# RWKV rounds of a decoder trunk on one core: the state's decay through TensorE, and more copies on ScalarE

## What is computed

```python
def rwkv7_recurrence(r, w, k, v, a, b, s0):
    def step(s, inp):
        r_t, w_t, k_t, v_t, a_t, b_t = inp
        sa = jnp.einsum('bhij,bhj->bhi', s, a_t)
        s = s * w_t[:, :, None, :] + sa[..., None] * b_t[:, :, None, :] + v_t[..., None] * k_t[:, :, None, :]
        return s, jnp.einsum('bhij,bhj->bhi', s, r_t)
...
y = ((y - mean) * lax.rsqrt(var + R_LN_EPS)).reshape(bsz, t, R_WIDTH) * ln_w + ln_b
bonus = jnp.sum(rh * kh * r_k, axis=-1, keepdims=True) * vh
y = y + bonus.reshape(bsz, t, R_WIDTH)
return (y * g) @ w_out, p[:, -1], s_fin
```

## Time and profile before

| | before |
|---|---|
| median of 3 runs | 4311.3 us (4311.24 to 4314.79) |
| the profiled execution's own time | 4307.08 us |
| its span from first to last instruction | 4305.3 us |
| granted clock of TensorE over the span | 0.963 |
| RWKV rounds in the span | about 2235 to 2850 us |
| busy in the span: PE, DVE, ACT | 92%, 57%, 35% |

### The profile page before, as it was taken

How to read it: one execution, slowest core, us unless ns; L and a number is a source line. 1 busy time by engine, 2 the same in 40 slices (tenths; PEclk the granted TensorE clock), 3 DMA queues, 4 the chain that set the end, 5 groups by cost and what they waited for, 6 DMA issues and landing times. The chain is left out here.

```text
span 4305.3 us, 84625 instructions
## 1 busy us (share of the span) xinstructions
PE 3955.7 (92%) x35797; PEld 3633.6 (84%) x35797; DVE 2449.4 (57%) x4964; ACT 1510.7 (35%) x2733; POOL 155.9 (4%) x153
## 2 busy tenths in 40 slices
PE   8799999999989999889968888869988899999998
PEld 4689999999988888889957777749868889999997
DVE  3345656332278886358857878746542464444446
ACT  2113232221177554334325545424521342111112
POOL 0000000000011111000000000000012000000000
PEclk9899999989999999999979999979999999999999
DMA  4323232243455554646631111042323031111102
GB/s 180 106 78 88 91 88 92 81 105 104 119 156 151 152 142 121 175 147 197 204 133 35 33 33 33 19 154 85 117 65 125 22 103 59 49 45 40 50 30 81
DMA packets 374279, 418.69 MB, mean 97 GB/s; under 512 B 49178, under 2 KB 315980, under 8 KB 373036
## 3 DMA queue, kind: packets, MB, share of 16 engines
q1 hardware_dynamic: 361615, 368.01, 28.1%
q0 software_dynamic: 7680, 27.97, 2.2%
q10 hardware_dynamic: 4608, 17.30, 1.0%
HBM read 289.10 MB, written 121.77 MB: 95 GB/s over the span
## 5 line engine op out<-in xcount | busy, mean ns | idle before, releaser
L245 PE MATMUL bank<-xn_hi,pw_whi 128*128 128x352 f32 (+1 forms) x2184 | 732.5, 335 | 20.5 <-PEq L54 8.8
L245 PE MATMUL bank<-xn_hi,pw_wlo 128*128 128x352 f32 (+1 forms) x2184 | 709.3, 325 | 0.0
L245 PE MATMUL bank<-xn_lo,pw_whi 128*128 128x352 f32 (+1 forms) x2184 | 708.8, 325 | 0.0
L245 PEld LDWEIGHTS bank<-xn_hi,pw_whi 128*128 128x128 f32 (+1 forms) x2184 | 414.8, 190 | 38.7 <-issue 24.4
L245 PEld LDWEIGHTS bank<-xn_lo,pw_whi 128*128 128x128 f32 (+1 forms) x2184 | 416.1, 191 | 3.3 <-issue 2.2
L245 PEld LDWEIGHTS bank<-xn_hi,pw_wlo 128*128 128x128 f32 (+1 forms) x2184 | 414.6, 190 | 1.3
L258 ACT ACTIVATE ring<-bank 128x352 f32<-128x352 f32 (+1 forms) x273 | 125.8, 462 | 502.2 <-PE bank L245 501.8
L3148 PE MATMUL bank<-bx_hi,bp_whi 128*128 128x384 f32 (+1 forms) x768 | 273.3, 356 | 30.9 <-DVE bx_lo L3206 18.3
L1797 PE MATMUL bank<-sum_x_hi,pw_whi 128*128 128x352 f32 x768 | 255.7, 333 | 38.7 <-DVE sum_x_lo L1776 23.2
L3769 PE MATMUL bank<-bx_hi,bp_whi 128*128 128x384 f32 (+1 forms) x768 | 251.3, 327 | 4.7 <-issue 4.7
L3769 PE MATMUL bank<-ml_hidden_hi,bp_whi 128*128 128x384 f32 (+1 forms) x768 | 254.5, 331 | 0.0
(11 more groups left out here) (687 smaller groups left out, 10415.9 us busy)
## 6 DMA issues: line engine op xcount, KB each, us to landing
ring<-in_w_in_dram SPq DMA_DIRECT2D x90, 512.0 KB, 4.8
proj_scratch<-ring SPq DMA_DIRECT2D x66, 528.0 KB, 2.9
m_seg<-acum_scratch SPq DMA_DIRECT2D x32, 512.0 KB, 6.8
ring<-in_mlp_w_dram SPq DMA_DIRECT2D x16, 1024.0 KB, 5.5
ring<-in_mlp_w_dram SPq DMA_DIRECT2D x32, 512.0 KB, 3.5
gates_scratch<-ring SPq DMA_DIRECT2D x24, 528.0 KB, 5.0
merged_scratch<-sum_gate ACTq DMA_DIRECT2D x24, 528.0 KB, 5.1
m_raw<-proj_scratch SPq DMA_DIRECT2D x24, 512.0 KB, 5.5
```

Source lines behind the costliest of these rows:

```text
L245: last = self.nc.tensor.matmul(ps[0:n, 0:m], w[:, q, 0:n], self.pair[x][:, q, t0:t0 + m], start=q == 0 and j == 0, stop=q == KD - 1 and j ...
```

## The change

In the scan the decayed state is no longer made by VectorE. TensorE adds eye x ST to the bank in which it accumulates K x V and B x U, and ScalarE takes the sum out, scaled by PC, as the new state. K x V moves from the chunk's first slot to its second. At a new head pair the products with the zero state are left out, with the memset. The copy SO goes to ScalarE, in front of its copy of y.

In the inversion the copies DY (of `square`) and F (of `turn`) go from VectorE to ScalarE, DY ahead of A2 and F ahead of G. In `Prepare` the shifted exponential is read from the unshifted one stored with a leading 1 (`ex`), so that one subtraction on VectorE and one exponential on ScalarE go; V is written by the token shift directly, without ScalarE's copy; the scaling with k_a becomes an activation in slot 6; the zeroing of `raw` comes in slot 6 of the round before. In `Finish` the mean is taken off by the product itself (`centre`), ScalarE squares and copies from PSUM, and two operations of VectorE are left for the affine step and the bonus, where there were three.

```diff
-             ("turn", "va"), ("cross1", "v"), ("cross2", "v"), ("cross3", "v")]
+             ("turn", "a"), ("cross1", "v"), ("cross2", "v"), ("cross3", "v")]
...
+        elif slot == 6:
+            act.wait_ge(self.a_ready, r + 1)
+            act.wait_ge(self.mixed, 3 * r + 3)
+            activation(T[7], T[2], ACT.Copy, scale=k.col["rwkv_k_a"][:, j:j + 1]).then_inc(self.a_scaled, 1)
         elif slot == 7:
             self.nc.scalar.preload_act_table_set("natural_log_exp_and_others")
             act.wait_ge(self.cum, r + 1)
-            activation(T[3], T[1], ACT.Exp, scale=-KAPPA)
+            activation(v.ex[:, :, 1:1 + RC], T[1].rearrange("p (c t) -> p c t", t=RC), ACT.Exp, scale=-KAPPA)
             activation(T[4], T[1], ACT.Exp, scale=KAPPA).then_inc(self.decays, 1)
...
-        elif slot == 9:
-            act.wait_ge(self.shifted, r + 1)
-            activation(T[0], T[0], ACT.Exp, scale=-KAPPA).then_inc(self.exps, 1)
-        elif slot == 18:
...
-            activation(v.V[:, r % 3, :, :], v.pm[:, 2, :].rearrange("p (c t) -> p c t", t=RC), ACT.Copy).then_inc(self.v_made, 1)
...
         if step == "square":
             dve.wait_ge(self.as_[p], evacuated(r, s - 1, "a"))
-            tt(x.DY[:, :, RC:2 * RC], x.D[:, :, :], mask(v.eye), ALU.add)
+            tt(x.DY[:, :, RC:2 * RC], x.D[:, :, :], mask(v.eye), ALU.add).then_inc(self.vs[p], 1)
+            return
...
-        elif step == "square":
-            last = copy(x.DY[:, :, 0:RC], view(b0))
...
-        elif step == "turn":
-            last = copy(x.F[:, :, :], view(b0))
...
         elif step == "square":
+            copy(x.DY[:, :, 0:RC], b0)
             last = copy(x.A2[:, :, :], b1)
...
         else:
+            copy(x.F[:, :, :], b0)
             last = copy(x.G[:, :, :], b1)
...
-                pe.wait_ge(self.s_off, self.updates(r, c))
-                pe.wait_ge(self.kx_mm, n + 1)
-                heads(mm, both[:, 0:RC], AR[:, 0:RC], ST, start=False, stop=True).then_inc(self.r_mm, 1)
-                swapped(mm, state[:, 0:RC], K, V, start=True, stop=False)
-                swapped(mm, o, V, KX[:, RC:2 * RC], start=True, stop=False).then_inc(self.kv_mm, 1)
+                if n % 16 == 0:
+                    swapped(mm, both[:, 0:RC], KX[:, 0:RC], V, start=True, stop=True).then_inc(self.r_mm, 1)
+                else:
...
+                    pe.wait_ge(self.s_off, self.updates(r, c))
+                    pe.wait_ge(self.kx_mm, self.carried(n))
+                    heads(mm, both[:, 0:RC], AR[:, 0:RC], ST, start=False, stop=True).then_inc(self.r_mm, 1)
+                    heads(mm, state[:, 0:RC], v.eye, ST, start=True, stop=False).then_inc(self.st_mm, 1)
+                swapped(mm, o, V, KX[:, RC:2 * RC], start=True, stop=False).then_inc(self.vk_mm, 1)
...
-        if slot == 0 and not w:
-            self.nc.vector.memset(now, 0.0).then_inc(self.s_off, 1)
...
+        elif c < 8 and sub == 2:
+            act.wait_ge(self.s_mm, 8 * r + c + 1)
+            self.nc.scalar.activation(v.ST[:, (c + 1) % 2, :], self.k.bank[1][:, 0:RC], ACT.Copy, scale=v.PC[:, r % 3, c:c + 1]).then_inc(self.s_off, 1)
         elif slot == 24:
+            if r % 2:
+                act.wait_ge(self.turned, r // 2 + 1)
...
+                self.nc.scalar.activation(v.SO[:, :], self.k.bank[1][:, 0:RC], ACT.Copy).then_inc(self.t_off, 1)
             act.wait_ge(self.read, 8 * r + 8)
```

More of the change, by code:

```diff
@@ L1037, in vector @@
         nc.vector.memset(v.reset[:, 0:RW:RC], 0.0)
+        nc.vector.memset(v.ex[:, :, 0:1], 1.0)
         dve.drain().then_inc(self.ones_made, 1)
-        nc.vector.tensor_scalar(v.rest[:, :], k.col["rwkv_mu"][:, 0:24], -1.0, 1.0, ALU.mult, ALU.add)
+        nc.vector.tensor_scalar(v.rest[:, 0:24], k.col["rwkv_mu"][:, 0:24], -1.0, 1.0, ALU.mult, ALU.add)
+        nc.vector.tensor_scalar(v.rest[:, 24:32], k.col["rwkv_k_a"], -1.0, 1.0, ALU.mult, ALU.add)
         for h in HEADS:
@@ L1183, in tensor, with scalar @@
             heads(self.nc.tensor.matmul, bank, v.ones, T[6], start=True, stop=True).then_inc(self.bon_sum, 1)
-    def scalar(self, act, r, slot, read):
+    def scalar(self, act, r, slot):
         if not 0 <= r < ROUNDS:
@@ L1239, in vector @@
             dve.wait_ge(self.scaled, 3 * r + slot - 2)
-            stt(out=pm[:, i, :], in0=raw[:, i, 1:1 + RW], scalar=v.rest[:, i * 8 + j:i * 8 + j + 1], in1=(T[1], D[1], D[2])[i],
+            if i == 2 and r >= 3:
+                dve.wait_ge(read, 8 * (r - 2))
+            stt(out=V if i == 2 else pm[:, i, :], in0=raw[:, i, 1:1 + RW], scalar=v.rest[:, i * 8 + j:i * 8 + j + 1], in1=(T[1], D[1], D[2])[i],
                 op0=ALU.mult, op1=ALU.add).then_inc(self.mixed, 1)
@@ L1244, in vector @@
             dve.drain()
+            if r % 2 and r + 1 < ROUNDS:
+                self.nc.vector.memset(raw[:, :, 0:1], 0.0).then_inc(self.zeroed, 1)
             self.nc.vector.tensor_tensor_scan(out=T[1], data0=v.reset[:, :], data1=T[0], initial=0.0, op0=ALU.mult, op1=ALU.add).then_inc(self.cum, 1)
[L1246 to L1251, removed]
         elif slot == 9:
-            dve.drain()
-            stt(out=T[7], in0=T[7], scalar=1.0, in1=pm[:, 1, :], op0=ALU.add, op1=ALU.mult)
+            dve.wait_ge(self.a_scaled, r + 1)
+            stt(out=T[7], in0=T[7], scalar=v.rest[:, 24 + j:25 + j], in1=pm[:, 1, :], op0=ALU.add, op1=ALU.mult)
         elif slot == 10:
@@ L1448, in tensor @@
                 heads(mm, both[:, 0:RC], N, v.R, start=True, stop=True).then_inc(self.u_mm, 1)
-                pe.wait_ge(self.kv_mm, n + 1)
-                heads(mm, o, ST, AR[:, RC:2 * RC], start=False, stop=False)
+                pe.wait_ge(self.vk_mm, n + 1)
+                if n % 16:
+                    heads(mm, o, ST, AR[:, RC:2 * RC], start=False, stop=False)
+                    pe.wait_ge(self.st_mm, self.carried(n))
+                elif r:
+                    pe.wait_ge(self.t_off, r // 2)
+                swapped(mm, state[:, 0:RC], K, V, start=n % 16 == 0, stop=False).then_inc(self.kv_mm, 1)
             else:
                 pe.wait_ge(self.u_off, n + 1)
+                pe.wait_ge(self.kv_mm, n + 1)
                 heads(mm, state[:, 0:RC], B, v.U, start=False, stop=True).then_inc(self.s_mm, 1)
@@ L1463, in vector @@
             return
[L1464 to L1485 removed]
+        v, c, sub = self.v, slot // 3, slot % 3
+        if c < 8 and sub == 0:
+            dve.wait_ge(self.r_mm, 8 * r + c + 1)
+            self.nc.vector.tensor_copy(v.R[:, :], self.k.bank[0][:, 0:RC]).then_inc(self.r_off, 1)
     def scalar(self, act, r, slot, stored):
@@ L1528, in tensor @@
             pe.wait_ge(y_off, r + 1)
-            heads(self.nc.tensor.matmul, bank, v.ones, v.y[:, r % 2, :], start=True, stop=True).then_inc(self.summed, 1)
+            heads(self.nc.tensor.matmul, bank, v.centre, v.y[:, r % 2, :], start=True, stop=True).then_inc(self.summed, 1)
         elif slot == 19:
@@ L1566, in scalar @@
         if slot == 17:
-            act.wait_ge(self.centred, r + 1)
-            self.nc.scalar.activation(v.F[0], v.y[:, r % 2, :], ACT.Square).then_inc(self.squared, 1)
+            act.wait_ge(self.summed, r + 1)
+            self.nc.scalar.activation(v.F[0], self.k.bank[7][:, :], ACT.Square).then_inc(self.squared, 1)
+            self.nc.scalar.activation(v.y[:, r % 2, :], self.k.bank[7][:, :], ACT.Copy).then_inc(self.centred, 1)
         elif slot == 20:
@@ L1626, in _ @@
                     scan.scalar(act, q - 1, slot, finish.stored)
-                    prepare.scalar(act, q + 1, slot, scan.read)
+                    prepare.scalar(act, q + 1, slot)
                     finish.scalar(act, q - 2, slot)
```

80 lines of the change are left out of this document (28 added, 52 removed).

## The result

| | before | after |
|---|---|---|
| median of 4 runs each | 4311.84 us (4311.24 to 4314.79) | 4258.31 us (4257.57 to 4263.01) |
| profiled execution's own time | 4307.08 us | 4258.98 us |
| its span | 4305.3 us | 4257.3 us |
| granted clock over the span | 0.963 | 0.966 |

The ratio is 0.9877, 95% interval 0.986 to 0.9894. The kernel is 53.5 us faster by the medians and 48.1 us by the profiled executions; forecast were 41.2.

A forecast was written before the change was run, and what follows sets the result against it. TensorE's walk through its slots, with its waits, was taken to bound the rounds. Terms -33.6, -4.5, +0.4 and -3.5 sum to -41.2 us on 4307.1; plus 4.2 to the median, about 4270 us, range 4246 to 4300.

The forecast's parts named there:

- Term 1: At a new head pair, dropping memset and zero-state products gains 4.8 us at each of seven transitions: -33.6 us.
- Term 2: In an ordinary round, four parts sum to -0.3 us, over fifteen rounds with a state: -4.5 us.
- The wait behind the table load: In each round TensorE waits for ScalarE's state of chunk 2, queued behind table load and copies: +1.0 us.
- F in front of G: In a round's last slots ScalarE's U for chunk 5 comes 0.27 later: +0.2 us a round.
- The late slots: Late in a round, TensorE's stops for the state and R go as VectorE's queue shortens: -1.9 us a round.
- Term 3: Ramp and tail of the rounds: +0.4 us for the ramp, -3.5 us for the tail.
- the tail: Last rounds, where the finish is alone: shorter finish, SO copy gone from VectorE, earlier R copy: -3.5 us.
- The ramp: First rounds: k_a scaling and longer inversion copies +1.4, first memset gone -1.0: +0.4 us.
- The transition stays long: Rival: at a pair's start SO, y, table load and U arrive last; two thirds of 5.2 us stay, 4296; chance 0.12.
- The new wait lowers the clock: Rival: TensorE's idling behind the table load lowers the clock each round, 48 us lost, 4318 us; chance 0.08.
- ScalarE's queue takes the state at each chunk: Rival: each chunk's state waits behind wide activations on ScalarE; at 0.6 us a chunk 4347; chance 0.06.
- TensorE alone is left: Rival: late waits and small gaps all go, a round is TensorE's busy time, about 31.5 us: 4246 us; chance 0.12.

The follow-up runs named there:

- e1: Kernel before with only the head pair's start changed (no zero-state products or memset, raw zeroed a round early): 4287.75 us, ratio 0.9936.
- e9: Kernel before with four extra pairs of 384 columns, results unused, where TensorE stands at a new head pair: 4302.56 us, ratio 0.9979.
- e14: Changed kernel with the DY copy alone back on VectorE, run again for a trace: 4253.42 us, ratio 0.9858.
- e11: Changed kernel with the F copy alone back on VectorE: 4258.38 us, ratio 0.9883.
- e7: Kernel before with the changed head pair's start and Finish, and SO on ScalarE; state, DY, F and Prepare as before: 4260.72 us, ratio 0.9881.
- e6: Changed kernel with the state made by VectorE again, without the product with eye: 4265.96 us, ratio 0.9892.
- e8: Changed kernel with the two exponentials one slot later and both copies, DY and F, back on VectorE: 4253.2 us, ratio 0.9855.
- e5: Kernel before with nine extra pairs of 384 columns, results unused, where TensorE stands at a new head pair: 4325.89 us, ratio 1.0027.

## Why the prediction was right, and what was off in it

The time lies in the range and on the forecast's side, 11.7 us below 4270. The sum of -41.2 splits by the trace into four stretches:

| stretch | forecast | measured |
|---|---|---|
| first to fourth scan instruction | about 0 | -1.8 |
| twelve intervals | 6 x 4.8 + 12 x 0.3 = -32.4 | -39.9 |
| sixteenth scan instruction to the next stage's table load | -4.8 - 0.6 - 3.5 = -8.9 | -9.3 |
| the rest of the program | 0 | +2.8 |

The third row is 94.88 us before and 85.61 after. ScalarE's timelines have its end, first of the kernel before, then of the changed one:

```profile
2850.41 1.28 ACT L3960 ACT_TABLE_LOAD   x1 [6.18 <-PEq L54]
```

```profile
2800.43 1.28 ACT L3954 ACT_TABLE_LOAD   x1 [5.68 <-PEq L54]
```

The last row is what is left of -48.1; the stages ahead of and behind the rounds are not changed. The error is in the twelve intervals, and in two terms.

**Term 1, the new head pair.** A transition cost 38.33 - 33.43 = 4.9 us before, and costs nothing now (32.28 against 32.83). The gain is 4.9 + 0.55 = 5.45 us each, above my upper bound of 5.2, where I took 4.8. The 0.4 that I held back for SO and y was not there: SO takes 0.22 us in ScalarE's queue, but TensorE's wait behind it is 0.26, and two products fewer stand on TensorE. 0.65 us, six times, is 3.9 of the 7.5 us that are missing. Two of the reasons behind the 4.8 need correcting. I wrote that nothing then distinguishes a long round from a short one but two products and the SO copy; e1 shows that the finish does, by 1.3 us, until it is shortened. And I had the slow clock as a second payment at every transition, of 3 us by the rival's price; e9 shows 2.0 us at three of six and 0.1 at the others, because the clock is low for some 7 us at the former only, and ScalarE's chain to U hides the first part of it. The term did not suffer from it, since it was taken from the mean of the long intervals and not from a price of the clock.

**Term 2, an ordinary round.** -0.3 forecast, -0.6 measured: the other 3.6 us. By parts:
- The wait behind the table load is there as described: 1.34 us in the row above, 18.6 us in 16 waits. I had DY's share in it as 2 x 0.28 = 0.56; e14 measures 0.57. The load takes 1.28 us and the exponential starts 1.30 us after the load's start (2522.74, 2524.04). The Trainium skill, "ScalarE: Activation LUTs", What ACT_TABLE_LOAD costs, gives 1283 ns for the load and 1380 ns more for a drain: the trace agrees with the first and shows nothing of the second.
- F in front of G was to cost 0.2; e11 shows no cost (1.4 us in twelve rounds the other way, within the disturbances).
- The late slots: their waits are gone, as forecast. But I credited nearly all of it to the state's move and 0.2 to the finish. e7 has the old state and the old copies, and its short rounds are down from 33.4 to 32.6, where e1, without the new finish, has 33.4: the finish is worth 0.8 us a round, and did by itself most of what I laid to the move. For the state's move my terms were +0.6 for the eye products, +0.4 for its share behind the load and -1.9 for the late slots, -0.9 in all; in this kernel it is worth 0.28 at most (e6). The step that failed is the mis-sizing of these two, -0.9 and -0.2 where 0.28 at most and 0.8 were measured, and with it the sentence "VectorE itself is relieved by some 8 us a round, but little of that is on the path". By the windows the relief is 158.2 / 200 x 35.9 - 136.0 / 200 x 32.6 = 6.2 us, and the microseconds of the finish in it, ahead of the state and of the new pair's first product, were on the path and were the gain. That the sum still came near is luck in part: too much for one move and too little for the other went into it.
- What the parts leave over stays open. State -3.4, DY +6.8 and F -1.4 make +2.0 us in twelve intervals between e7 and the changed kernel; measured is -0.15. The missing -2.1 could be `Prepare`'s changes, which no run tried alone, the place of K x V, the "issue" waits (1.2 us in e7, 3.2 in the changed kernel), or that the parts do not add up.

**Term 3.** The stretch with the tail, the last rounds, was right within half a microsecond (-8.9, -9.3), but it holds a transition and two ordinary rounds too. At their measured gains, 5.45 and 1.2, they leave -2.6 for the tail where -3.5 was forecast: two errors that cancel. The ramp, the first rounds, was off by about 2 us; I have not looked further into it.

**The rivals.** *The transition stays long* is out by the intervals; two thirds of seven times 5.2 would be 24 us, not 26. *The new wait lowers the clock*: stops of up to 1.34 us, about one a round, left the granted clock at 1.00 in every window of 4 us from 2264 to 2768. In the window 2525 to 2528, right behind the stop, TensorE was busy for 2.01 of 3 us:

```profile
2525.00:2528.00 3.00, 2.01 (x62) 2.01 (x64) 1.51 (x5) 2.59 (x8) 0.00 (x0) 1.00 0.00 0
```

*ScalarE's queue takes the state at each chunk* is out: TensorE's waits for ScalarE's state are 16 in some 14 rounds, about one a round, where the rival needed one in every chunk. *TensorE alone is left* came nearer than I gave it: TensorE is busy for 185 of 200 us, and in e8 for 189. Its own sum has 1.6 us a round where 33.0 - 31.5 is 1.5.

## What to carry to other kernels

Before pricing a move of work between engines, try what the source engine does when only its unneeded work goes: here the start of a pair and a shorter finish gave all of the gain in the twelve intervals, and the rest of the change, the state, two copies and `Prepare`, gave none taken together, though DY's move costs and the state's likely pays. An engine that is idle for half of the time can still be a bad host for a copy: DY joined ScalarE's queue ahead of the table load and again behind it, and made each round 0.57 us longer. A low clock behind a stall costs only what is not hidden by the next late engine: fill the stall with idle products once, and read the difference stall by stall, since the mean of 1.06 us here was 2.0 at three stalls and next to nothing at three.

## What was not expected of the hardware

- A pair of 64x64 x 384 products on two opposite quarters takes 0.64 us: two passes 0.32 apart, with both quarters starting within 0.01 us of each other. TensorE's timeline of e5:

```profile
2496.99 0.48 PE L1128 MATMUL bank<-r_reset,r_eye 64*64 64x384 f32 x1
2497.00 0.48 PE L1129 MATMUL bank<-r_reset,r_eye 64*64 64x384 f32 x1
2497.32 0.48 PE L1128 MATMUL bank<-r_reset,r_eye 64*64 64x384 f32 x1
```

- With four such pairs in each stop of some 3.5 us (e9) the granted clock stayed at 1.00; without them stops of 3.2 us were followed by some 7 us at 0.50 at three transitions and by some 3.5 us at the other three.
